# Four small gaps between the activation tiles of a two-block transformer kernel: what the on-chip addresses of matmul operands do to its time

## The chip, the cores and the metric

The kernel runs on one core of one Trainium2 chip, as one launch. The metric is the device time of that launch in microseconds (us), the median of the runs shown. Beside it stands one execution recorded by the hardware profiler, from which all rows below are read.

## What is computed

The reference runs two small transformer stacks, one behind the other, on 256 tokens of width 1024, all in float32. The first has two layers, each with two gated feed-forward layers (FFN) around a mixer (a short convolution in layer 0, a three-branch sparse attention in layer 1). The second has two layers with a mixer each.

```python
def swiglu_ffn(x, w_in, w_out):
    gate, up = jnp.split(x @ w_in, 2, axis=-1)
    return (jax.nn.silu(gate) * up) @ w_out
...
    for i in range(DEPTH):
        if i == N_A_LAYERS:
            kv = shared_kv(h, kv_norm, w_kv, k_norm, ...)
        h = h + 0.5 * swiglu_ffn(rmsnorm(h, ffn1_norm[i]), ffn1_w_in[i], ffn1_w_out[i])
        hn = rmsnorm(h, mix_norm[i])
        if i < N_A_LAYERS:
            h = h + short_conv_mixer(hn, conv_w_in[i], conv_w[i], conv_w_out[i])
        else:
            h = h + nsa_mixer(hn, attn_w_q[j], attn_q_norm[j], attn_w_o[j], rel_bias, kv)
        h = h + 0.5 * swiglu_ffn(rmsnorm(h, ffn2_norm[i]), ffn2_w_in[i], ffn2_w_out[i])
...
    for layer in range(DEPTH):
        h = rms_norm(x, pre_norm[layer])
        m = even_mixer(...) if layer % 2 == 0 else odd_mixer(...)
        x = x + rms_norm(m, post_norm[layer])
```

The feed-forward width is 2816, so each of the four FFNs multiplies 256 x 1024 by 1024 x 5632 and 256 x 2816 by 2816 x 1024. Every other large product (`conv_w_in`, `w_kv`, `attn_w_q`, `w_in_even`, `w_in_odd` and the matching output matrices) has 1024 rows too.

## The kernel before

The activations stay on the chip for the whole program, features on the partitions and tokens along the free axis: `hres` holds the residual as 8 tiles of 128 x 256. The weights are streamed from device memory, each once, through two rings of two slots: `raw_a` for the input matrices (a chunk is 1024 x 256), `raw_b` for the rows of the output matrices (a chunk is 128 x 1024).

**Three products for one.** TensorE takes its operands as fp32r, which keeps fewer bits than float32. To keep the precision, each operand is split into a high part (a rounded copy) and a low part (the rest). The weights are split on the chip: ScalarE writes `wah` (line 1098) and `wbh` (1105), VectorE writes `wal` (1494, 1665), and GpSimd writes `wbl` (2046; VectorE at 1749 in the mixers). The activations are split as well: ScalarE writes `hnh` (1166), VectorE `hnl` (1512, 1548), `hidh` (1547) and `hidl` (1548). One product is then three matmuls, which the helper `mm3` issues on lines 644 to 646:

```python
mm(dst, wh, xh, start=start, stop=False)   # L644: high weights, high activations
mm(dst, wh, xl, start=False, stop=False)   # L645: high weights, low activations
return mm(dst, wl, xh, start=False, stop=stop)  # L646: low weights, high activations
```

Here the weights are the stationary operand, 128 x 128 each, loaded afresh for each matmul by a LDWEIGHTS; the activations are the moving operand, 128 x 256. So in each triple TensorE reads a 512-byte stretch of each partition of a weight tile, and streams a 1024-byte stretch of an activation tile. In the jobs of kind "N" of the projections the roles are exchanged: `hnh`/`hnl` are stationary and `wah`/`wal` are moving.

**An FFN** has 22 chunks. For each, `up` makes gate and up parts (2 groups x 8 row tiles, 16 triples) from `hnh`, `hnl`, `wah`, `wal` into PSUM bank 4 or 5, and `down` adds one chunk of hidden features to the residual's 8 accumulators (8 triples) from `hidh`, `hidl`, `wbh`, `wbl`. `up` of a chunk goes ahead of `down` of the chunk before. That is 24 triples, or 72 matmuls, a chunk. Between them VectorE scales the sums (1600), ScalarE applies silu (1204), and VectorE multiplies (1604) and splits (1547, 1548). The convolution has the same form with 8 chunks. The projections (`project`) run `mm3` over 5 to 16 chunks; attention (`attend`) works with plain float32 matmuls (832, 833, 850 to 852, 868, 869), with two more bf16 matmuls on a tile of zeros (874) at each step of the first attention. All waits are semaphores between hand-written engine programs; there is no scheduler.

**Where the tiles stand.** On-chip tensors are declared with the helper `sb(...)` at the top of `build`. They are placed in that order from byte 16,512 of each partition on, and each start is rounded up to a multiple of 32 bytes. The weight tiles come early, the split activations late: `wah`, `wal`, `wbh`, `wbl`, `hres`, `sqs`, `cst`, `arena`, `t384`, ..., `tmp`, `gate_hid`, then `hidh`, `hidl`, `hnh`, `hnl`, and behind them `zero`, `rms`, `pbuf`, `ptb` and the small tiles of the softmax.

Of the kernel before, what the change touches and what calls it, by code (L numbers as in the profile page):

```python
# [18 lines left out]
F32R = mybir.dt.float32r  # L19
# [6 lines left out]
P = 128  # L26
T = 256
D = 1024
KT = D // P
# [72 lines left out]
def build(nc, a, out):  # L102
    ctx = ExitStack()
    with ctx:
        def sb(name, shape, dt=F32):
            return ctx.enter_context(nc.sbuf_tensor(name, shape, dt))
# [38 lines left out]
        tmp = sb("tmp", [P, 2, 512])  # L145
        gate_hid = sb("gate_hid", [P, 4, T])
        silu, hf = gate_hid[:, 0:2], gate_hid[:, 2:4]
        hidh, hidl = sb("hidh", [P, 2, T], F32R), sb("hidl", [P, 2, T], F32R)
        hnh, hnl = sb("hnh", [P, KT, T], F32R), sb("hnl", [P, KT, T], F32R)
        zero = sb("zero", [P, 512], BF16)  # L150
        rms = sb("rms", [P, T + 2])
        rtok, rln = rms[:, 0:2], rms[:, 2:T + 2]
# [2006 lines left out]
```

## Time and profile before

| | us |
|---|---|
| runs of the kernel before | 1530.22, 1530.47, 1540.99 |
| their median | 1530.47 |
| the profiled execution's own time | 1530.22 |
| its span, from the first to the last instruction | 1528.1 |
| TensorE busy with matmuls in the span | 1428.9 |
| VectorE, ScalarE, GpSimd busy | 900.4, 631.7, 435.2 |

The profiled execution is one of the three runs. Its time is its span and 2.1 us around it. Engines run at the same time, so their busy times don't add up. PE is TensorE's matmul row, PEld its weight loads, DVE is VectorE, ACT is ScalarE, POOL is GpSimd. Matmuls are pipelined, so that one of some 280 ns starts every 113 to 118 ns; what a matmul costs in a dense stretch is the distance between two starts, not its own duration.

### The profile page before, as it was taken

What the parts mean: (1) busy time and instruction counts of PE and PEld (TensorE: products, weight loads), DVE (VectorE), ACT (ScalarE), POOL (GpSimd) and SP (SyncE); (2) the same over time, 40 slices, a digit from 0 to 9 for tenths busy, and PEclk for the clock granted to TensorE, in tenths of its full rate; (3) what the DMA queues carried; (4) which work ended last, traced back from release to release, by engine and by line L of the source; (5) the groups of instructions that cost most, each with busy time, mean ns of one, the idle gap of its engine ahead of it and who ended that gap; (6) DMA issues with size and microseconds to landing.
All of it is one profiled execution on the core that took longest, in us unless ns stands there. A gap on an engine that the chain in (4) does not pass through costs nothing.

```text
span 1528.1 us, 28008 instructions
## 1 busy us (share of the span) xinstructions
PE 1428.9 (94%) x10980; PEld 1319.2 (86%) x11011; DVE 900.4 (59%) x1406; ACT 631.7 (41%) x954; POOL 435.2 (28%) x226
## 2 busy tenths in 40 slices
PE   4999999999999999999979999999999998799767
PEld 4999999989999989999965557999999986698646
DVE  3784568775455554545665663745455696573764
ACT  3443353354334353434434553534342434434442
POOL 1354431124443414444213440344430003000310
PEclk8999999999999899999976999999999997999788
DMA  7778646657765456666330102666643541353002
GB/s 205 209 211 236 191 140 191 178 181 233 218 184 174 125 159 188 183 188 183 124 104 23 32 22 70 196 186 196 200 143 99 164 145 34 123 166 111 28 1 83
DMA packets 271773, 222.55 MB, mean 146 GB/s; under 512 B 8082, under 2 KB 252326, under 8 KB 271580
## 3 DMA queue, kind: packets, MB, share of 16 engines
q1 hardware_dynamic: 268176, 212.44, 45.9%
q0 software_dynamic: 2368, 7.60, 2.2%
q10 hardware_dynamic: 1164, 1.62, 0.3%
q8 instruction: 43, 0.70, 0.2%
q14 instruction: 22, 0.18, 0.0%
HBM read 216.40 MB, written 4.19 MB: 144 GB/s over the span
## 4 chain that ended last, share of the span: by engine, by line
PE 77%; DVE 13%; ACT 5%; DMA 2%; issue 2%; ACTq 0%; another core or an unknown queue 0%; DVEq 0%; SPq 0%
PE bank L644 21%; PE bank L645 20%; PE bank L646 20%; PE bank L832 2%; DVE wal L1494 2%; PE bank L874 2%; PE bank L868 2%; DVE rstd L1476 2%; ACT wah L1098 1%; DVE wal L1665 1%; PE bank L833 1%; PE bank L850 1%; ACT hnh L1166 1%; DMA raw_a<-in_ffn_w_in 1%; PE bank L911 1%
## 5 line engine op out<-in xcount | busy, mean ns | idle before, releaser
L644 PE MATMUL bank<-hnh,wah 128*128 128x256 f32 (+1 forms) x2080 | 589.1, 283 | 8.5 <-DVE wal L1494 6.4
L2046 POOL TENSOR_TENSOR wbl<-raw_b,wbh 128x1024 fp32r<-128x1024 f32 x102 | 337.7, 3312 | 883.4 <-ACT wbh L1105 787.5
L645 PE MATMUL bank<-hnl,wah 128*128 128x256 f32 (+1 forms) x2080 | 581.0, 279 | 0.0
L646 PE MATMUL bank<-hnh,wal 128*128 128x256 f32 (+1 forms) x2080 | 580.8, 279 | 0.0
L644 PEld LDWEIGHTS bank<-hnh,wah 128*128 128x128 f32 (+1 forms) x2080 | 395.6, 190 | 10.3 <-issue 4.0
L645 PEld LDWEIGHTS bank<-hnl,wah 128*128 128x128 f32 (+1 forms) x2080 | 393.3, 189 | 2.1 <-issue 1.4
L646 PEld LDWEIGHTS bank<-hnh,wal 128*128 128x128 f32 (+1 forms) x2080 | 393.6, 189 | 0.0
L1494 DVE TENSOR_TENSOR wal<-raw_a,wah 128x2048 fp32r<-128x2048 f32 (+1 forms) x129 | 297.8, 2308 | 121.8 <-ACT wah L1098 120.9
L1098 ACT ACTIVATE wah<-raw_a 128x2048 fp32r<-128x2048 f32 (+3 forms) x127 | 239.0, 1885 | 85.5 <-PE bank L646 63.8
L644 PE MATMUL bank<-hidh,wbh 128*128 128x256 f32 x768 | 216.4, 282 | 2.0 <-DVE hidl L1548 2.0
L1204 ACT ACTIVATE gate_hid<-tmp 128x256 f32<-128x256 f32 x88 | 36.9, 419 | 426.8 <-DVE tmp L1600 426.8
L645 PE MATMUL bank<-hidl,wbh 128*128 128x256 f32 x768 | 213.3, 278 | 0.0
L646 PE MATMUL bank<-hidh,wbl 128*128 128x256 f32 x768 | 213.2, 278 | 0.0
L1600 DVE TENSOR_TENSOR tmp<-bank,rms 128x512 f32<-128x512 f32 x88 | 60.9, 692 | 220.1 <-PE bank L646 210.8
L1105 ACT ACTIVATE wbh<-raw_b 128x1024 fp32r<-128x1024 f32 x120 | 125.6, 1049 | 62.5 <-PE bank L646 37.6
L644 PEld LDWEIGHTS bank<-hidh,wbh 128*128 128x128 f32 x768 | 145.3, 189 | 2.4 <-DVE hidl L1548 2.4
L645 PEld LDWEIGHTS bank<-hidl,wbh 128*128 128x128 f32 x768 | 144.2, 188 | 0.4
L646 PEld LDWEIGHTS bank<-hidh,wbl 128*128 128x128 f32 x768 | 144.3, 188 | 0.0
L2118 POOL TENSOR_SCALAR pbuf<-pbuf,rs 128x256 f32<-128x256 f32 (+1 forms) x72 | 64.0, 889 | 88.0 <-DVE rs L1722 63.8
L1315 ACT ACTIVATE pbuf<-pbuf,nmx 128x128 f32<-128x128 f32 (+2 forms) x144 | 59.5, 415 | 41.3 <-DVE nmx L1707 35.3
L1604 DVE TENSOR_TENSOR gate_hid<-gate_hid,tmp 128x256 f32<-128x256 f32 x88 | 39.9, 453 | 42.9 <-ACT gate_hid L1204 42.9
L832 PE MATMUL bank<-arena 64*128 64x256 f32 (+1 forms) x112 | 47.1, 533 | 18.8 <-DVEq L1947 8.8
(237 smaller groups left out, 1827.5 us busy)
## 6 DMA issues: line engine op xcount, KB each, us to landing
raw_a<-in_ffn_w_in SPq DMA_DIRECT2D x176, 512.0 KB, 5.1
raw_b<-in_ffn_w_out SPq DMA_DIRECT2D x88, 512.0 KB, 4.8
raw_a<-in_w_in_even SPq DMA_DIRECT2D x15, 1024.0 KB, 5.3
raw_a<-in_conv_w_in SPq DMA_DIRECT2D x24, 512.0 KB, 4.3
raw_a<-in_w_in_odd SPq DMA_DIRECT2D x11, 1024.0 KB, 5.3
raw_a<-in_w_kv SPq DMA_DIRECT2D x6, 1024.0 KB, 5.0
raw_b<-in_conv_w_out SPq DMA_DIRECT2D x8, 512.0 KB, 5.7
raw_a<-in_attn_w_q SPq DMA_DIRECT2D x4, 1024.0 KB, 5.9
```

What stands on the lines that cost most here:

```text
L644: mm(dst, wh, xh, start=start, stop=False)
L645: mm(dst, wh, xl, start=False, stop=False)
L646: return mm(dst, wl, xh, start=False, stop=stop)
L832: mm(b[:, 0:T], m["q"][:, P:T], m["k"], start=True, stop=True)
L1098: act.activation(wah[:, s, :, 0:w], raw_a[:, wa.slot(u), :, 0:w], ACT.Copy).then_inc(S("a_hi"), 1)
L1105: act.activation(wbh[:, s], raw_b[:, s], ACT.Copy).then_inc(S("b_hi"), 1)
L1315: x = act.activation(pbuf[:, r, lo:hi], pbuf[:, r, lo:hi], ACT.Exp, bias=nmx[:, r, i:i + 1], accum_out=sm[:, r, i:i + 1])
L1494: v.tensor_tensor(wal[:, s, :, 0:w], raw_a[:, (n["ra"] + u) % 2, :, 0:w], wah[:, s, :, 0:w].bitcast(F32), ALU.subtract).then_inc(S("a_lo"), 1)
L1600: v.tensor_tensor(tmp[:, gs, :].rearrange("p (g c) -> p g c", g=2), bank[4 + gs][:, :].rearrange("p (g c) -> p g c", g=2), rln[:, None, :] ...
L1604: link(v.tensor_tensor(hf[:, hs, :], silu[:, gs, :], tmp[:, gs, T:2 * T], ALU.mult))
L2046: g.tensor_tensor(wbl[:, s], raw_b[:, s], wbh[:, s].bitcast(F32), ALU.subtract).then_inc(S("b_lo"), 1)
L2118: g.tensor_scalar(pbuf[:, r, lo:hi], pbuf[:, r, lo:hi], rs[:, r, 1:2], None, ALU.mult).then_inc(S("p1_scaled"), 1)
```

## The change

Four tensors that nothing reads or writes are declared between the split activations. They take 64, 96, 32 and 384 bytes of each partition.

```diff
-        hidh, hidl = sb("hidh", [P, 2, T], F32R), sb("hidl", [P, 2, T], F32R)
-        hnh, hnl = sb("hnh", [P, KT, T], F32R), sb("hnl", [P, KT, T], F32R)
+        sb("gap0", [P, 16])
+        hidh = sb("hidh", [P, 2, T], F32R)
+        sb("gap1", [P, 24])
+        hidl = sb("hidl", [P, 2, T], F32R)
+        sb("gap2", [P, 8])
+        hnh = sb("hnh", [P, KT, T], F32R)
+        sb("gap3", [P, 96])
+        hnl = sb("hnl", [P, KT, T], F32R)
```

No instruction is added, removed or moved on any engine; only start addresses differ. These are the starts in bytes of each partition in the two built programs, and their distances to the weight tiles. The four weight tiles all start at 128 bytes past a multiple of 2048, so one distance serves for all four.

```
tile            before    after     distance to the weight tiles, modulo 2048
wah              41088    41088
wal              57472    57472
wbh              73856    73856
wbl              82048    82048
hidh            187200   187264     704 before,  768 after
hidl            189248   189408     704 before,  864 after
hnh             191296   191488     704 before,  896 after
hnl             199488   200064     704 before, 1280 after
zero            207680   208256
rms             208704   209280
pbuf            209760   210336
ptb             220512   221088
```

Within these tiles the reads step by 512 bytes (stationary blocks) and 1024 bytes (moving tiles), so what stays fixed is the distance modulo 512: 192 bytes for all four before, and 256, 352, 384 and 256 bytes after. Every tensor behind `hnl` stands 576 bytes (9 x 64) later. These tiles do not move and come up in the prediction: `hres` at 90240, `cst` at 100480, `arena` at 110752, `t384` at 155808, `tmp` at 179008, `gate_hid` at 183104.

## Rows read from the trace of the kernel before

**Rows 1.** The page's head: busy time of each engine, its share and instructions

```profile
span 1528.1 us, 28008 instructions
PE 1428.9 (94%) x10980; PEld 1319.2 (86%) x11011; DVE 900.4 (59%) x1406; ACT 631.7 (41%) x954; POOL 435.2 (28%) x226
```

**Rows 2.** The chain of work that ended last, shares of the span

```profile
PE 77%; DVE 13%; ACT 5%; DMA 2%; issue 2%; ACTq 0%; another core or an unknown queue 0%; DVEq 0%; SPq 0%
```

**Rows 3.** Costliest groups of TensorE by form: shape, count | busy us, mean ns | idle before, releasers

```profile
L644 PE MATMUL bank<-hnh,wah 128*128 128x256 f32 x2064 | 584.6, 283 | 7.5 <-DVE wal L1494 6.4 <-DVE wal L1665 1.0
L645 PE MATMUL bank<-hnl,wah 128*128 128x256 f32 x2064 | 576.5, 279 | 0.0
...
L644 PE MATMUL bank<-hidh,wbh 128*128 128x256 f32 x768 | 216.4, 282 | 2.0 <-DVE hidl L1548 2.0
L645 PE MATMUL bank<-hidl,wbh 128*128 128x256 f32 x768 | 213.3, 278 | 0.0
...
L645 PE MATMUL bank<-hnl,wbh 128*128 128x256 f32 x192 | 53.9, 280 | 0.0
```

**Rows 4.** Busy time by stretch: steady parts of the four FFNs, then the attention stages

```profile
60.00:200.00 140.00, 140.00 (x1238) 140.00 (x1237) 86.55 (x106) 55.29 (x55) 66.01 (x25) 1.00 0.73 212
340.00:480.00 140.00, 140.00 (x1237) 140.00 (x1237) 71.97 (x87) 55.31 (x53) 61.08 (x18) 1.00 0.71 212
580.00:740.00 160.00, 160.00 (x1361) 160.00 (x1360) 77.58 (x95) 59.23 (x57) 67.40 (x19) 1.00 0.62 187
980.00:1120.00 140.00, 140.00 (x1238) 140.00 (x1237) 72.79 (x86) 54.82 (x52) 63.42 (x18) 1.00 0.66 199
782.00:930.00 148.00, 136.41 (x616) 77.25 (x626) 89.57 (x300) 71.23 (x252) 53.01 (x62) 0.86 0.09 28
```

**Rows 5.** TensorE's groups in the third FFN, 580 to 740 us

```profile
L646 PE MATMUL bank<-hnh,wal 128*128 128x256 f32 x302 | 84.9, 281 | 0.0
L645 PE MATMUL bank<-hidl,wbh 128*128 128x256 f32 x152 | 42.7, 281 | 0.0
```

**Rows 6.** TensorE's groups in the first FFN, 60 to 200 us

```profile
L646 PE MATMUL bank<-hnh,wal 128*128 128x256 f32 x276 | 76.2, 276 | 0.0
L645 PE MATMUL bank<-hidl,wbh 128*128 128x256 f32 x137 | 37.8, 276 | 0.0
```

**Rows 7.** The same in two neighbouring stretches of the convolution, 256:265 and 268:288 us

```profile
L645 PE MATMUL bank<-hnl,wah 128*128 128x256 f32 x19 | 5.2, 276 | 0.0
...
L645 PE MATMUL bank<-hnl,wah 128*128 128x256 f32 x41 | 11.5, 281 | 0.0
```

**Rows 8.** Timeline, float32 matmuls back to back: start, us to the last end, count

```profile
33.27 1.89 PE L628 MATMUL bank<-arena,cst 128*128 128x256 f32 x8
...
1372.05 2.32 PE L1038 MATMUL bank<-arena,t 128*96 128x256 f32 x10
```

**Rows 9.** Length of one such matmul at line 1038, from its line's view

```profile
L1038 PE MATMUL bank<-arena,t x32: 379/379/379, 1372.1 to 1378.7; 128*96 128x256 f32 x32
```

**Rows 10.** VectorE's groups by form: three of 512 columns on tiles of different starts, and the splits

```profile
L1600 DVE TENSOR_TENSOR tmp<-bank,rms 128x512 f32<-128x512 f32 x88 | 60.9, 692 | 220.1 <-PE bank L646 210.8 <-PE bank L652 6.0 <-DVE wal L1494 1.5
L1548 DVE TENSOR_TENSOR hidl<-gate_hid,hidh 128x256 fp32r<-128x256 f32 x96 | 40.9, 426 | 3.3
...
L1538 DVE TENSOR_TENSOR arena<-bank,rms 128x512 f32<-128x512 f32 x28 | 19.4, 691 | 20.4 <-PE bank L646 18.9 <-DVE rms L1484 0.7
...
L1585 DVE TENSOR_TENSOR hres<-hres,tmp 128x512 f32<-128x512 f32 x8 | 5.5, 692 | 0.3
```

## The prediction

> **What bounds the kernel now.** I read the page's head first: TensorE has a matmul under way in 1428.9 of 1528.1 us, the next engine, VectorE, in 900.4 [rows 1]. The chain of work that ended last says the same from the other end: 77% of the span stands on TensorE, 13% on VectorE [rows 2]. The groups of TensorE show on what: the triples of lines 644 to 646, with `hnh`/`hnl` against `wah`/`wal` (2064 triples), with `hid` against `wb` (768) and with `hn` against `wb` (192), and almost no idle time ahead of them, 7.5 and 2.0 us in the two largest groups [rows 3]. With the 128 triples of the projections that have the roles exchanged and 16 narrow ones, that is about 3 x 3,150 = 9,450 matmuls. Whatever changes the distance between two of their starts by 1 ns changes the time by 9.5 us. The change can act there, because every one of these matmuls reads an activation tile whose distance to the weight tiles is new.
>
> **The pace of these matmuls.** The view by stretch gives it. In the steady parts of three FFNs 1,238, 1,237 and 1,238 matmuls stand in 140 us; the count takes in some two that began before the stretch, so a start comes every 140 / 1,235.5 = 113.3 ns. In the third FFN 1,361 stand in 160 us: 160 / 1,358.5 = 117.8 ns [rows 4]. The clock was granted in full in all four. So there are two paces, 4.5 ns apart. They also show in the duration of one: 281 ns in the third FFN [rows 5], 276 ns in the first [rows 6]. That makes a mean a ruler: over the whole program the low-part matmuls of `down` average 278 ns [rows 3], so (278 - 276) / (281 - 276) = 40% of them ran at the slow pace.
>
> **What the trace says of addresses.** Three readings bear on it.
>
> First, the four FFNs use the same tiles at the same addresses, and three have the fast pace and one the slow [rows 4]. In the convolution one stretch has 276 ns and the next 281 ns, again with the same tiles [rows 7]. So the pace is a state that a stretch falls into when it starts, and the distance between tiles does not decide it, at least not alone.
>
> Second, within a stretch the pace does not depend on which tiles are read. `up` and `down` read different tiles, and the stationary block steps by 512 bytes against a moving tile that stays. Both have 281 ns in the slow stretch [rows 5] and both have 276 ns in the fast one [rows 6]. This covers steps of 512 bytes and more. It does not cover finer ones: all four activation tiles now stand at 192 bytes modulo 512 from the weights, and the change moves them to 256, 352, 384 and 256.
>
> Third, for fine distances the nearest rows are float32 matmuls. Line 628 streams `sqm` (in `arena`, tile 36, byte 147,616) against the ones in `cst` (byte 100,992): 46,624 bytes, 32 modulo 128. Eight take 1.89 us from the first start to the last end. Line 1038 streams `dq` (in `arena`, tile 16, byte 127,136) against blocks of `uq` (`t384`, from byte 155,808 in steps of 384): 28,672 bytes and more, in steps of 384, always 0 modulo 128, as `hidh`, `hnh` and `hnl` will have it. Ten take 2.32 us [rows 8]. With 379 ns for the last one [rows 9], the starts lie (1.89 - 0.38) / 7 = 216 ns and (2.32 - 0.38) / 9 = 216 ns apart. A moving stream with weight loads beside it goes at one speed at both distances. The weight load has more time to hide there than in a triple (216 ns against 113), so this is evidence and no proof.
>
> **The change part by part.** The two programs have the same instructions in the same order, so there is no count of added work.
> - *The triples.* Value taken: 0 ns each, from the three readings. Bounds: if all of them took the slow pace, the 60% that are now fast would pay 4.5 ns: 0.6 x 9,450 x 4.5 = +25.5 us. If all took the fast pace: 0.4 x 9,450 x 4.5 = -17.0 us. Still lower lies the float32 pass: 216 ns for a float32 matmul of 256 columns that streams them twice is 108 ns a pass, and against the mean of 0.6 x 113.3 + 0.4 x 117.8 = 115.1 that would be 9,450 x 7.1 = -67 us. Nothing shows a triple at that pace, so I keep it as the far end only.
> - *VectorE and ScalarE on the moved tiles.* Value taken: 0. A tensor_tensor of 512 columns takes 692 ns into `tmp` (byte 179,008, 64 modulo 128), 691 ns into `arena` (32 modulo 128) and 692 ns into `hres` (0 modulo 128) [rows 10], so the start's place modulo 128 does not matter to 1 ns. `hidl` at 32 modulo 64 is new, and `arena` has it already. Bounds: 1 ns either way over 300 instructions of the attention window on VectorE [rows 4], or 0.3 us. In the FFNs the split of 426 ns [rows 10] lies beside TensorE, which has no pause there in 140 us [rows 4].
> - *Tiles behind the gaps.* `pbuf`, `ptb`, `zero` and the small ones move by 576 bytes, a multiple of 64. TensorE reads `pbuf`, `ptb` and `zero` in attention; by rows 8 again 0.
>
> Sum: 1528.1 + 2.1 around the span + 0 = 1530.2 us, against a median of 1530.47 of the three runs.
>
> **What a run does by itself.** The sum would hold if the stages drew the same paces again. An FFN has 22 x 72 = 1,584 matmuls, so one that changes pace moves the time by 1,584 x 4.5 ns = 7.1 us. The profiled execution has one slow FFN of four. The run of 1540.99 us is 10.8 us longer than the profiled one, as much as one and a half FFNs. If the pace is drawn anew by each stretch, at 40% slow, the expected count is 1.6 of four, 0.6 more than profiled, or +4 us; two of three runs drew the better one. I take half of that: 1532 us.
>
> **Two places of the Trainium skill.** Its page "TensorE: Matmul & The Clock Gate", section "Back-to-back issue gap", puts the warm distance of two matmuls at N / 2.4 + 2.5 ns, an estimate of 109.2 ns for 256 columns. By that rule 4.1 ns a matmul is lost to something even at the fast pace, and a layout that gave it back would be worth some 39 us more than the fast rival below: 1474 us. The trace has no triple that fast, the loads being afresh each time. Against it speaks "SBUF — State Buffer", section "Who interferes with whom": TensorE has one read port for the moving operand and an independent one for LDWEIGHTS. By this rule no distance can matter, and the sum stays at 1530 us. The equal 216 ns of rows 8 agree with it; that the two paces exist at all is not explained by it.
>
> **The rivals.**
> 1. *Slower: the two read streams meet.* The mechanism is in the triples: the slow pace is the load of one block and the stream of another held up at the same part of the memory, and a distance of 0 modulo 128 makes it permanent. It decides where `hidh`, `hnh` and `hnl` come to stand at such a distance (768, 896, 1280), which is all of them but `hidl`. All triples at 117.8 ns: 1530.2 + 25.5 = 1556 us. For it: a slow pace exists, and 0 modulo 128 is untested in triples. Against it: rows 8 at the same distance, and the slow pace's presence at 192 modulo 512, where it comes and goes.
> 2. *Faster: the common distance was the bad one.* With four different distances the streams no longer fall into step and each stretch takes the fast pace: 1530.2 - 17.0 = 1513 us. For it: all four tiles share one distance now, so a stretch that falls into step stays so for 1,440 matmuls. Against it: three of four FFNs have the fast pace at that distance.
> 3. *No lasting effect, but a worse draw.* Three or four slow FFNs in the middle run: 1530.2 + 3 x 7.1 = 1552 us. It needs two of three runs to be so.
>
> **How the numbers follow.** No effect of the layout, with the draw near that of before: 0.74, at 1532 us, its own range 1522 to 1546. Rival 1: 0.11. Rival 2, with its far end by the float32 pass: 0.10. Rival 3: 0.05. The range of 1517 to 1549 holds nearly all of the first case and the near edges of the rivals, and leaves out the 1556 and the 1513. A measurement of this kernel can tell about 1% from no change, which is 15 us: 1515 to 1546. Slower by more than that is most of rivals 1 and 3 (0.14); faster is rival 2 at full size (0.09); within 1% the rest (0.77).
>
> **What would show it right or wrong.** Right: the four FFN stretches show 1,237 or 1,238 matmuls in 140 us, or about 1,189 (140 / 117.8), and nothing else; some have the one and some the other; L1600 and the splits keep 692 and 426 ns; idle time ahead of L644 stays under 10 us. Wrong, rival 1: all four FFNs at 281 ns, and in a repeat as well. Wrong, rival 2: no stretch at 281 ns, the projections included. Wrong in kind: a third pace, say 109 or 122 ns, or a pace that differs between `up` and `down` within one stretch, since that could only come from the distances.

## The result, and the profile after

The changed kernel takes 1562.48 us (median of 4 runs, 1562.28 to 1564.36). The kernel before, run again beside it, has 1535.73 us (4 runs, 1530.22 to 1543.82). The ratio is 1.0165, with a 95% interval of 1.0124 to 1.0206: slower, by 1.65%, and outside the range of the forecast (1517 to 1549). Medians here and below are of all runs, while ratios and their intervals leave out slow runs, those over 1.5% above the fastest of the same kernel. The profiled execution took 1562.44 us, with a span of 1560.3, which is 32.2 us more than before.

The page's head, the chain's shares and the costliest groups of TensorE by form, of the changed kernel (its lines stand 6 later: L650 to L652 are the triple of L644 to L646):

```profile
span 1560.3 us, 28039 instructions
PE 1466.3 (94%) x11011; PEld 1351.9 (87%) x11011; DVE 899.3 (58%) x1406; ACT 631.1 (40%) x954; POOL 435.4 (28%) x226
...
PE 81%; DVE 11%; ACT 4%; DMA 2%; issue 2%; ACTq 0%; DVEq 0%; SPq 0%
```

```profile
L650 PE MATMUL bank<-hnh,wah 128*128 128x256 f32 x2064 | 593.8, 288 | 2.5 <-DVE wal L1500 2.1 <-DVE wal L1671 0.4
L652 PE MATMUL bank<-hnh,wal 128*128 128x256 f32 x2064 | 586.6, 284 | 0.0
L651 PE MATMUL bank<-hnl,wah 128*128 128x256 f32 x2064 | 581.9, 282 | 0.0
L650 PE MATMUL bank<-hidh,wbh 128*128 128x256 f32 x768 | 218.6, 285 | 2.7 <-DVE hidl L1554 2.7
```

TensorE alone has grown: VectorE, ScalarE and GpSimd are busy as long as before to 1.1 us [rows 1], and TensorE's share of the chain went from 77 to 81% [rows 2]. The `hnh,wah` group averages 288 ns for 283 [rows 3], and the idle time ahead of it fell from 7.5 to 2.5 us, since a slower TensorE is waited for more and waits less. The 31 matmuls more in the count are records that the trace of before lacks.

The stretches of the four FFNs (columns: stretch, its length, PE, PEld, DVE, ACT and POOL busy with counts, granted clock, DMA share, GB/s):

```profile
60.00:200.00 140.00, 140.00 (x1182) 140.00 (x1181) 82.61 (x102) 52.93 (x54) 62.37 (x24) 1.00 0.69 203
340.00:480.00 140.00, 140.00 (x1181) 140.00 (x1181) 70.35 (x85) 53.91 (x51) 59.22 (x17) 1.00 0.69 206
600.00:760.00 160.00, 160.00 (x1351) 160.00 (x1350) 78.38 (x95) 60.31 (x57) 66.09 (x19) 1.00 0.60 180
1010.00:1150.00 140.00, 140.00 (x1182) 140.00 (x1181) 67.86 (x84) 52.44 (x50) 56.79 (x16) 1.00 0.61 184
```

Against 1,238 in 140 us before [rows 4] there are 1,182: 140 / 1,179.5 = 118.7 ns from start to start, and the same in all four. No stretch has 113.3 ns. Within a stretch, `up` and `down` now differ, which they did not before [rows 5, 6]. The groups of the first FFN, 60 to 200 us:

```profile
L652 PE MATMUL bank<-hnh,wal 128*128 128x256 f32 x262 | 74.2, 283 | 0.0
L651 PE MATMUL bank<-hnl,wah 128*128 128x256 f32 x261 | 73.3, 281 | 0.0
L651 PE MATMUL bank<-hidl,wbh 128*128 128x256 f32 x133 | 37.3, 280 | 0.0
```

The starts in the trace give `up` 119.1 ns and `down` 118.0 ns. Summed over all starts of triples that lie 100 to 150 ns apart, they are 15.6 us over an even 113.33 ns a matmul before, and 51.6 us after. That is +36.0 us in the triples; the pauses between them shrink by 4.7 us, and what remains (+0.9 us) lies outside. So the 32.2 us are found, and the added time lies in the matmuls whose operands the gaps moved.

VectorE paid nothing as a whole. Its rows of 512 columns and the split on the moved tile (512 columns at L1606 and L1544, the split at L1554):

```profile
L1606 DVE TENSOR_TENSOR tmp<-bank,rms 128x512 f32<-128x512 f32 x88 | 60.9, 692 | 244.1 <-PE bank L652 236.2 <-PE bank L658 5.5 <-DVE wal L1500 0.8
L1554 DVE TENSOR_TENSOR hidl<-gate_hid,hidh 128x256 fp32r<-128x256 f32 x96 | 40.9, 426 | 3.3
L1544 DVE TENSOR_TENSOR arena<-bank,rms 128x512 f32<-128x512 f32 x28 | 19.3, 691 | 22.1 <-PE bank L652 20.6 <-DVE rms L1490 0.7
```

All three are as in [rows 10], to the nanosecond. One row on a moved tile does differ, the rounded copy into `hidh`, before and after:

```profile
L1547 DVE CAST hidh<-gate_hid 128x256 fp32r<-128x256 f32 x96 | 34.5, 359 | 8.9
...
L1553 DVE CAST hidh<-gate_hid 128x256 fp32r<-128x256 f32 x96 | 36.4, 379 | 8.9
```

The 20 ns do not go with the address: in the kernels further down the same row has 380 ns with `hidh` at its old byte (hid_undone) and 336 ns with it at the changed kernel's byte (hn_undone). TensorE has no pause there.

### The profile page after: what moved, and what is told of

It reads as the page before. It is cut to its first block, busy times and chain, and to the rows that moved or that the text cites. A ratio compares the mean times of both kernels' runs of the same rounds, so it can differ in the third digit from the quotient of the medians.

```text
span 1560.3 us, 28039 instructions
## 1 busy us (share of the span) xinstructions
PE 1466.3 (94%) x11011; PEld 1351.9 (87%) x11011; DVE 899.3 (58%) x1406; ACT 631.1 (40%) x954; POOL 435.4 (28%) x226
## 4 chain that ended last, share of the span: by engine, by line
PE 81%; DVE 11%; ACT 4%; DMA 2%; issue 2%; ACTq 0%; DVEq 0%; SPq 0%
PE bank L650 22%; PE bank L652 22%; PE bank L651 21%; PE bank L838 2%; DVE wal L1500 2%; PE bank L880 2%; PE bank L874 2%; DVE rstd L1482 2%; ACT wah L1104 1%; PE bank L839 1%; PE bank L856 1%; PE bank L875 1%; DMA raw_a<-in_ffn_w_in 1%; PE bank L877 1%; PE bank L917 1%
## 5 line engine op out<-in xcount | busy, mean ns | idle before, releaser
L650 PE MATMUL bank<-hnh,wah 128*128 128x256 f32 (+1 forms) x2080 | 598.3, 288 | 3.4 <-DVE wal L1500 2.1
L652 PE MATMUL bank<-hnh,wal 128*128 128x256 f32 (+1 forms) x2080 | 591.1, 284 | 0.0
L650 PEld LDWEIGHTS bank<-hnh,wah 128*128 128x128 f32 (+1 forms) x2080 | 395.8, 190 | 8.5 <-issue 3.7
L652 PEld LDWEIGHTS bank<-hnh,wal 128*128 128x128 f32 (+1 forms) x2080 | 393.6, 189 | 0.0
L650 PE MATMUL bank<-hidh,wbh 128*128 128x256 f32 x768 | 218.6, 285 | 2.7 <-DVE hidl L1554 2.7
L652 PE MATMUL bank<-hidh,wbl 128*128 128x256 f32 x768 | 215.2, 280 | 0.0
L1606 DVE TENSOR_TENSOR tmp<-bank,rms 128x512 f32<-128x512 f32 x88 | 60.9, 692 | 244.1 <-PE bank L652 236.2
L650 PEld LDWEIGHTS bank<-hidh,wbh 128*128 128x128 f32 x768 | 144.8, 189 | 3.1 <-DVE hidl L1554 3.1
L652 PEld LDWEIGHTS bank<-hidh,wbl 128*128 128x128 f32 x768 | 145.0, 189 | 0.0
```

Source lines behind the costliest of these rows:

```text
L1606: v.tensor_tensor(tmp[:, gs, :].rearrange("p (g c) -> p g c", g=2), bank[4 + gs][:, :].rearrange("p (g c) -> p g c", g=2), rln[:, None, :] ...
```

## The experiments

Two kinds of kernel were run: the whole network with another layout, timed against the kernel before in the same session, and a measuring program that leaves the network out and runs only TensorE stretches at chosen distances (distance: start of the moving tile less start of the stationary block, in bytes). Each measuring program was executed once. The main loop of the first measuring program:

```python
for i, (wo, xo) in enumerate(SWEEP):        # element offsets; their difference is the distance
    if i:
        pe.wait_ge(given, i)                # one small ScalarE copy between two stretches
    for n in range(COUNT):
        m = mm(b, w[:, wo:wo + P], x[:, xo:xo + T], start=n == 0, stop=n == COUNT - 1)
    m.then_inc(asked, 1)
```

### Distance or start address: pace_curve, shift_all, weights_moved

> A measuring program: it leaves out the whole network. After a warm-up, TensorE runs 128 stretches of 48 fp32r matmuls (128x128 stationary, 128x256 moving), each stretch with one fixed byte distance between the stationary block and the moving tile: 0 to 2016 bytes in steps of 32, in a mixed order, first with the stationary block at byte 32,896, then 96 bytes later. Theory A (the distance between the two read streams sets the pace): the start-to-start time of a stretch is a function of the distance, some values at 113 ns and others at 118 to 123 ns, and the two halves give the same function; 704 is among the fast ones, 768, 864, 896 and 1280 among the slow ones. Theory B (the moving tile's own start address sets it): the second half's curve is that of the first moved by 96 bytes. Theory C (the draw at the start of a stretch alone, as forecast): 113.3 or 117.8 in no order, with no relation between the halves.

The timeline of five stretches, each cut off inside (start, us to the last end, count). In this order: distance 704, 896, 768, 864, and 1280, the last with the stationary block 96 bytes later:

```profile
219.57 3.93 PE L70 MATMUL bank<-x,w 128*128 128x256 f32 x32
307.17 3.96 PE L70 MATMUL bank<-x,w 128*128 128x256 f32 x32
382.27 4.00 PE L70 MATMUL bank<-x,w 128*128 128x256 f32 x32
425.99 3.88 PE L70 MATMUL bank<-x,w 128*128 128x256 f32 x31
482.28 3.88 PE L70 MATMUL bank<-x,w 128*128 128x256 f32 x31
```

With 0.28 us for the last matmul: 3.65 / 31 = 117.7 ns at 704, 3.68 / 31 = 118.7 at 896, 3.72 / 31 = 120.0 at 768, 3.60 / 30 = 120.0 at 864 and 1280. The whole curve, in ns from start to start, is the same eight numbers over and over from 0 to 2016 bytes:

```
distance modulo 256      0    32    64    96   128   160   192   224
block at byte 32,896   120.0 117.8 117.8 120.0 118.7 117.3 117.8 118.3
block at byte 32,992   120.0 116.7 117.8 120.0 118.7 117.3 117.8 118.3
```

(Mean of the last 40 starts of a stretch; each of the eight repeats in eight periods within 0.1 ns.) The distance sets the pace, and it counts modulo 256. The start address by itself does little: of the sixteen values only the one at 32 differs between the halves, by 1 ns. Of theory A one part failed: 704 showed 117.8 and not 113.3.

shift_all, against the kernel before:

```diff
+        sb("gap", [P, 48])
         raw_a = sb("raw_a", [P, 2, KT, T])
```

> One gap of 192 bytes ahead of the first tensor, the four gaps left out: all tiles stand 192 bytes later, all distances stay at 704 modulo 2048, and hnh starts at the very byte (191,488) where the changed kernel has it. Theory A (distance): as the kernel before, 1530 to 1544 us, FFN stretches at 113.3 or 117.8 ns. Theory B (own start address): the triples with hnh go to about 120 ns as in the changed kernel, 1550 to 1562 us.

Measured: 1533.40 us (10 runs, 1529.29 to 1548.15), ratio 0.9995 (0.9963 to 1.0026). Theory A holds: `hnh` at the very byte of the changed kernel costs nothing as long as the weights moved along. The FFN stretches show the two paces of before; the first and the third:

```profile
60.00:200.00 140.00, 140.00 (x1238) 140.00 (x1237) 87.00 (x106) 55.21 (x55) 66.72 (x25) 1.00 0.72 214
...
600.00:740.00 140.00, 140.00 (x1191) 140.00 (x1190) 67.53 (x84) 52.02 (x50) 58.20 (x17) 1.00 0.62 187
```

weights_moved, against the kernel before:

```diff
+        w2k = sb("w2k", [P, P])
+        w2v = sb("w2v", [P, 64])
+        rb = sb("rb", [33, 16])
         raw_a = sb("raw_a", [P, 2, KT, T])
...
-        rb = sb("rb", [33, 16])
...
-        w2k = sb("w2k", [P, P])
-        w2v = sb("w2v", [P, 64])
```

> w2k, w2v and rb (832 bytes) are declared ahead of the weight tiles and not behind them: the weights start 832 bytes later, the activations at the same bytes as in the kernel before; all four distances become 1920 modulo 2048, which is 896 modulo 1024, hnh's in the changed kernel. Theory A (distance): the pace of the triples rises to about 120 ns in up and down alike, 1570 to 1580 us (9,450 x 5 ns more than before). Theory B (own start address of the moving tile): as the kernel before, 1530 to 1544 us.

Measured: 1560.84 us (4 runs, 1559.91 to 1574.53), ratio 1.0196 (1.0126 to 1.0265). The split activations had not moved by a byte, and the triples slowed all the same. The pace was forecast a little too high (about 120 ns, and so 1570 us at least); the FFN stretch shows 118.7 ns, which is the curve's value at 128 modulo 256:

```profile
60.00:200.00 140.00, 140.00 (x1182) 140.00 (x1181) 82.43 (x102) 52.94 (x54) 61.99 (x24) 1.00 0.71 203
```

### Where the 113.3 ns come from: pace_phase

> The measuring program again, with the network left out: 192 stretches of 34 fp32r matmuls; distances 0 to 240 bytes in steps of 16, each tried behind 12 different leading float32 matmuls (none, or 2 to 512 columns), so that the stretch starts at another moment against the chip's clocks. The first curve has a period of 256 bytes and gave 117.8 ns at 192, where the kernel before has both 113.3 and 117.8. Theory A2 (distance and the start's moment together set the pace): 192 shows both 113.3 and 117.8 ns, depending on the leading matmul; 0, 96 and 128 never fall under 118 ns. Rival (the float of 113.3 comes from something else in the real kernel, such as the alternation of tiles): 192 stays at 117.8 behind every lead.

A lead is the float32 matmul that runs just ahead of a stretch. The timeline of three stretches, cut off inside: distance 192 with no lead, 192 behind a lead of 2 columns, 112 behind a lead of 190 columns:

```profile
51.82 2.88 PE L73 MATMUL bank<-x,w 128*128 128x256 f32 x24
...
126.41 2.75 PE L73 MATMUL bank<-x,w 128*128 128x256 f32 x22
...
650.82 2.66 PE L73 MATMUL bank<-x,w 128*128 128x256 f32 x22
```

That is 2.60 / 23 = 113.0, 2.47 / 21 = 117.6 and 2.38 / 21 = 113.3 ns. Over the 12 leads, distance 192 had the fast pace 6 times and the slow one 6 times, with nothing between: theory A2 holds in this, and the two paces are those that the kernel before has in its stretches. What picks one of the two is not known: with no lead, this program and pace_fine have 113.3 ns at 192, while pace_curve, with no lead either, has 117.8 ns in all its 16 stretches at 192 modulo 256. Distances 0, 96 and 128 never fell under 118.5. One distance had the fast pace behind all 12 leads: 112, which no 32-byte rounding of starts would hit. The others of the 16 lay between 116.6 and 120.2.

### Gaps that are multiples of the period: gaps_256

Against the changed kernel:

```diff
-        sb("gap0", [P, 16])
+        sb("gap0", [P, 64])
         hidh = sb("hidh", [P, 2, T], F32R)
-        sb("gap1", [P, 24])
+        sb("gap1", [P, 64])
         hidl = sb("hidl", [P, 2, T], F32R)
-        sb("gap2", [P, 8])
+        sb("gap2", [P, 64])
         hnh = sb("hnh", [P, KT, T], F32R)
-        sb("gap3", [P, 96])
+        sb("gap3", [P, 128])
         hnl = sb("hnl", [P, KT, T], F32R)
```

> Four gaps again, but of 256, 256, 256 and 512 bytes: larger in all than those of the change, and they leave each distance at 192 modulo 256. If the distance counts modulo 256 (the measured curve's period), nothing changes: 1530 to 1544 us, triples at 113.3 or 117.8 ns. If the cost of the change came from the tiles being apart at all, from four different distances, or from the tiles behind them standing later: 1550 us or more.

Measured: a median of 1547.14 us (10 runs, 1530.00 to 1560.05), ratio 1.0015 (0.9958 to 1.0072), while the kernel before had 1539.45 in that session, up to 1554.23. The median lies between the two ranges that were expected, 3 us over the first; by the ratio, gaps twice as large in all as those of the change make no difference that can be told. The run-to-run spread is that of before, and so are the paces: two FFNs fast (1,238 in 140 us, the first like the second) and two slow (1,360 in 160 us and 1,191 in 140 us). The second to the fourth:

```profile
340.00:480.00 140.00, 140.00 (x1238) 140.00 (x1237) 71.95 (x87) 55.28 (x53) 61.02 (x18) 1.00 0.70 213
580.00:740.00 160.00, 160.00 (x1360) 160.00 (x1360) 78.45 (x95) 60.30 (x57) 66.30 (x20) 1.00 0.60 183
990.00:1130.00 140.00, 140.00 (x1191) 140.00 (x1190) 67.44 (x81) 50.73 (x48) 60.52 (x17) 1.00 0.61 185
```

### Undoing one half: hid_undone and hn_undone

Both against the changed kernel. First hid_undone:

```diff
-        sb("gap0", [P, 16])
         hidh = sb("hidh", [P, 2, T], F32R)
-        sb("gap1", [P, 24])
         hidl = sb("hidl", [P, 2, T], F32R)
-        sb("gap2", [P, 8])
+        sb("gap2", [P, 48])
         hnh = sb("hnh", [P, KT, T], F32R)
         sb("gap3", [P, 96])
```

> The changed kernel with hidh and hidl back at their bytes of before (192 modulo 256 from the weights); hnh, hnl and all tiles behind them stay exactly where the change puts them. If each tile's own distance counts, the triples with hnh/hnl keep their 119 to 120 ns and only the down triples (2,304 matmuls at 118.0 ns in the changed kernel) can fall to 113 to 118 ns: 1551 to 1562 us. If the two gaps at hid carry the cost (hidl is the one tile that starts at an odd multiple of 32 bytes): 1530 to 1544 us.

Measured: 1565.01 us (4 runs, 1562.53 to 1579.86), ratio 1.0201 (1.0142 to 1.0260). Nothing came back, not even the 0 to 7 us allowed for. `down`, though its two tiles were at 192 again, ran at 118.0 ns in the first FFN, as in the changed kernel (118.0). It starts behind an `up` of 48 matmuls at bad distances; its first two starts lie 123 ns apart, and then it keeps the slow pace of 192 (117 to 119 ns from start to start). The group of its low-part matmuls in the first FFN, with the 281 ns of the slow pace:

```profile
L649 PE MATMUL bank<-hidl,wbh 128*128 128x256 f32 x131 | 36.8, 281 | 0.0
```

Then hn_undone:

```diff
         sb("gap0", [P, 16])
         hidh = sb("hidh", [P, 2, T], F32R)
         sb("gap1", [P, 24])
         hidl = sb("hidl", [P, 2, T], F32R)
-        sb("gap2", [P, 8])
+        sb("gap2", [P, 24])
         hnh = sb("hnh", [P, KT, T], F32R)
-        sb("gap3", [P, 96])
         hnl = sb("hnl", [P, KT, T], F32R)
```

> The other half: hidh and hidl stay where the change puts them (768 and 864), hnh and hnl return to 192 modulo 256. If the costs of the tiles add up, this kernel pays what the first half did not: at most 2,304 matmuls x 3 ns = 7 us over the kernel before, 1537 to 1546 us. If the fast pace needs every tile of the stream at a good distance (each down breaks it for the up behind it), the FFN stretches stand at 117.8 ns throughout and only the convolution's and projections' long up stretches draw 113.3: 6,336 FFN matmuls x 4.5 ns x the share that was fast before, 1550 to 1560 us.

Measured: 1540.73 us (10 runs, 1538.85 to 1545.07), ratio 1.0000 (0.9971 to 1.0028). The time agrees with the additive branch, the mechanism with neither. The stretches of the first and of the third FFN:

```profile
60.00:200.00 140.00, 140.00 (x1206) 140.00 (x1206) 84.75 (x105) 55.47 (x55) 62.36 (x25) 1.00 0.72 210
...
600.00:740.00 140.00, 140.00 (x1206) 140.00 (x1205) 69.56 (x85) 53.90 (x51) 58.04 (x18) 1.00 0.63 190
```

All four have 1,206: 140 / 1,203.5 = 116.3 ns, a pace that no FFN of the kernel before shows. The starts give `down` 117.8 and `up` 115.6 on the mean. But no single `up` has 115.6: whole `up`s of 48 matmuls alternate, 113.4 ns in one and 117.7 in the next, without an exception in the four stretches. Two neighbours in the first FFN, 98.2 to 103.2 us and 106.5 to 111.6 us:

```profile
L650 PE MATMUL bank<-hnl,wah 128*128 128x256 f32 x15 | 4.1, 276 | 0.0
...
L650 PE MATMUL bank<-hnl,wah 128*128 128x256 f32 x15 | 4.2, 281 | 0.0
```

These are the two paces of distance 192. So behind each `down` at bad distances the `up` takes one of them anew, here in strict turns, and keeps it to its end. An FFN no longer stays at one pace, and the spread is smaller: 1538.85 to 1545.07 us in 10 runs with a granted clock of 0.949 to 0.957. The kernel before, in its ten runs of the session with a clock of 0.948 or more, had 1532 to 1544 us in nine and 1558 in one. By the sums over 113.33 ns a matmul, one execution each: before 15.6 us, hid gaps alone 27.5, hn gaps alone 51.7, both 51.6. The parts don't add up (12 and 36 us, and 36 together); the `hn` gaps have the whole cost by themselves.

### Pairs of distances: pace_triples

> The measuring program with the network's own triples (high weights with high activations, high with low, low with high; the block steps by 512 bytes per triple): all 81 pairs of distances for the high and the low activation tile out of 0, 32, 64, 96, 112, 128, 160, 192, 224 bytes, each behind two leads. If a triple's pace is the sum of what the single distances gave (two for the high tile, one for the low): 113.4 at (112, 112), 113.4 or 117.8 at (192, 192), 120 at (0, 96), 118.6 to 120 at (128, 0). If what one matmul loses shifts the next one against its load, the mixed pairs depart from that: the network shows 118.0 at (0, 96) where the sum says 120, and 119.1 at (128, 0); the program should then show the network's numbers.

In ns from start to start, mean of the last 21 matmuls of a stretch, first lead and second lead:

```
high, low distance:  (192,192)      (112,112)      (0,96)         (128,0)        (0,0)          (112,192)
                     113.3, 113.3   113.3, 113.3   117.8, 117.8   120.0, 120.0   120.0, 120.0   115.6, 115.6
```

Of 81 pairs only two have 113.3 ns, those with both tiles at 192 and both at 112, and one more stays at 115.6 behind both leads. At (0, 96), the changed kernel's `hid` tiles, the mean of the single distances would be 120 and the program has 117.8, as the network's `down` (118.0). So the pace of a triple is not the mean of its single distances. At (128, 0), `hn`'s, it has 120.0 against the network's 119.1; that `down` breaks in there is a likely reason, not a tested one. Two matmuls that lie 21 starts apart, at (192, 192) and at (0, 96), both with the first lead:

```profile
144.92 0.28 PE L79 MATMUL bank<-x,w 128*128 128x256 f32 x1
147.30 0.28 PE L79 MATMUL bank<-x,w 128*128 128x256 f32 x1
...
164.10 0.28 PE L79 MATMUL bank<-x,w 128*128 128x256 f32 x1
166.57 0.28 PE L79 MATMUL bank<-x,w 128*128 128x256 f32 x1
```

That is 2.38 / 21 = 113.3 and 2.47 / 21 = 117.6 ns.

### What takes part: pace_fine

> The measuring program: distances 0 to 248 bytes in steps of 8 behind three leads; then a stationary block of 64 columns in place of 128 at steps of 16; then plain float32 matmuls. If two read streams hinder each other, the extra over the best pace (up to 6.7 ns at a distance of 0) shrinks to about half with half the block to read, and keeps its dependence on the distance; float32 matmuls, whose load has twice the time to hide in, stay at 216 ns at all distances. If the extra comes from the moving tile alone, it stays as large with 64 columns, and float32 shows it twice (about 229 ns at 0).

The timeline of three stretches, cut off inside: a block of 64 columns at distance 0, the same at 192, plain float32 at 0:

```profile
491.83 2.88 PE L78 MATMUL bank<-x,w 128*64 128x256 f32 x24
...
509.75 3.02 PE L78 MATMUL bank<-x,w 128*64 128x256 f32 x24
...
639.72 5.56 PE L80 MATMUL bank<-x,w 128*128 128x256 f32 x25
```

Three readings. With plain float32 matmuls the rows started 215.8 ns apart at all 16 distances ((5.56 - 0.38) / 24 here; each matmul has two rows). With a block of 64 columns the range stayed (113.3 to 120.0 ns), but the curve was another: 113.3 at 0, where 128 columns have 120.0, and 119.0 at 192, where they have 113.3 in this program. This fits neither branch: the extra did not halve, and it cannot come from the moving tile alone, since only the stationary block had changed. And the 16 distances that are odd multiples of 8 bytes had 120 ns or more in nearly all of their 48 stretches: one has 118.2, the others 119.8 to 130.3.

### A layout at the fast distance: at_112

```diff
-        hidh, hidl = sb("hidh", [P, 2, T], F32R), sb("hidl", [P, 2, T], F32R)
-        hnh, hnl = sb("hnh", [P, KT, T], F32R), sb("hnl", [P, KT, T], F32R)
+        split_x = sb("split_x", [P, 44 + 20 * T], F32R)[:, 44:44 + 20 * T].rearrange("p (a t) -> p a t", t=T)
+        hidh, hidl, hnh, hnl = split_x[:, 0:2], split_x[:, 2:4], split_x[:, 4:12], split_x[:, 12:20]
```

> All four activation tiles start 176 bytes later than before, 112 modulo 256 from the weights, the distance that gave 113.4 ns behind every lead. If the curve holds in the network, every stretch of triples runs at 113.3 ns: the 40% of slow ones before gain 17 us against the profiled 1530, so 1512 to 1516 us, with a spread under 3 us from run to run. If the curve is one of the measuring program alone (one block read again and again), it stays at 1530 to 1560 us.

Measured: 1525.27 us (10 runs, 1520.84 to 1536.19), ratio 0.9926 (0.9888 to 0.9964). It beats both kernels, the one before by 0.7%, and in the profiled execution every FFN has the fast pace; the first and the third:

```profile
60.00:200.00 140.00, 140.00 (x1237) 140.00 (x1237) 86.91 (x106) 55.24 (x55) 67.21 (x25) 1.00 0.73 213
...
580.00:740.00 160.00, 160.00 (x1414) 160.00 (x1414) 80.05 (x98) 60.81 (x59) 71.34 (x20) 1.00 0.63 191
```

It is some 10 us short of what I expected, and its spread is 15 us, not 3. Two parts are found. In the triples 5.2 us over the even 113.33 ns are left, so the profiled execution gained 10.4 us there and not 17. Some of that lies in the jobs of kind "N", where the roles are exchanged: they now have the weights 144 modulo 256 behind the blocks, and ran at up to 120.0 ns (in the kernel before, at 64, they ran at 117.8). Some lies behind each pause, where the first ten starts or so are 113 to 120 ns apart before the fast pace is found. And the runs differ in the granted clock: 0.949 to 0.954 in the seven under 1528 us, 0.941 to 0.946 in the three at 1535 to 1536 us. So a second source of spread goes with the clock; only one of the ten runs has a trace, so the paces of the others are not known.

## Why the prediction was wrong

**What bounds the kernel, and what 1 ns is worth: right.** TensorE's triples set the end before and after, and 3.9 ns more a matmul (115.0 to 118.9 on the mean) made +36 us, of which the pauses gave back 5.

**The step that failed: "The triples. Value taken: 0 ns each".** It measured +3.9 ns each. The three readings under it were true as rows and did not carry the conclusion.
- The first, that the pace is a state that a stretch falls into "and the distance between tiles does not decide it, at least not alone": pace_phase shows that the same tiles can have two paces at 192. But that is a property of this distance (others, such as 16 and 128, have two paces as well, but both slow). At 0, 96 or 128 no stretch with a 128-column block had the fast pace. Two outcomes at one distance said nothing of other distances.
- The second, no difference between `up` and `down` and between steps of 512 bytes: the period is 256, so each comparison made there was one of a distance with itself. I had written that it does not cover finer steps, and then counted it as one of three readings for zero all the same. The kernel before had one other distance to look at: in the jobs of kind "N" the exchanged roles put the moving weights at 64 modulo 256. The five stretches there of more than 30 matmuls, 256 columns and full clock all ran at 117.8 ns, never at 113.3.
- The third, float32 rows at 0 modulo 128: pace_fine confirms it at 16 distances, and it does not carry over to the triples. The likely reason is that the load there has 216 ns to hide in and here no time to spare, as the last rows of this section show; no run tests it. One row was also read as one matmul: line 1038 issues 16 matmuls and has 32 rows, so a float32 matmul takes two rows of 216 ns. No triple of 256 moving columns had a pace under 113.3 ns in any run, so nothing bears out the far end of 108 ns.

**The rival that came true: the first, in the main.** "All triples at the slow pace", +25.5 us and 1556 us, is 6 us short of the 1562.48. It had the right sign and the right place, and a chance of 0.11. Its condition was off: not a distance of 0 modulo 128, but nearly any modulo 256 (only 112 and 192 showed the fast pace with 128-column blocks). So was its price: 118.9 ns on the mean and not 117.8, since other distances have paces of their own. The sign announced in the text, "a third pace [...] or a pace that differs between `up` and `down` within one stretch", is what the profile shows.

**The second rival: wrong for this change, right as a possibility.** There is a layout with the fast pace in every FFN, at_112. The distances of the change are not it: of the pairs tried, only those with both tiles at 112 or both at 192 have the fast pace.

**The draw of each run: supported, and not the whole of the spread.** Layouts with all tiles at 192 modulo 256 were profiled three times, with one slow FFN at 1530.22 us, one at 1533.86 (shift_all) and two at 1540.40 (gaps_256). And runs of the kernel before at the same granted clock still differ: 1532.41 us at 0.954 and 1542.49 at 0.955 in the session of hn_undone. The run of 1540.99 us itself has no trace. The 1532 us was a guess at the middle; the medians of the later sessions were 1535 to 1542. In at_112 the times go with the granted clock over 15 us, so not all of the spread is the draw.

**VectorE and the tiles behind the gaps: right, 0.** Rows of 692, 691 and 426 ns stayed, and the one that did not, the copy into `hidh`, does not follow the address. All that lies outside the triples and their pauses is +0.9 us, and gaps_256, with the tiles behind moved by 1,280 bytes, is at 1.0015.

**On the two places of the Trainium skill.** The rule of "SBUF — State Buffer", section "Who interferes with whom", that the moving operand and LDWEIGHTS have independent read ports, would leave no room for a distance to matter, as the prediction read it. The measured curve differs (113.3 to 120.0 ns in pace_phase, in stretches in which no other engine has more than one small copy), and the measurement decides. Whether it is the reads that meet is open, as said below. The 109.2 ns that "TensorE: Matmul & The Clock Gate", section "Back-to-back issue gap", gives for 256 columns were not met at any of the distances tried; the best is 113.3. That section gives its formula for a single matmul apart and says that it does not hold for a stream with loads, so the prediction's 1474 us had little to stand on.

**What stays open.** That the distance between the stationary block and the moving tile, modulo 256 bytes, sets the pace is shown: by the curve, by weights_moved and by shift_all. Why is not, and neither is what picks one of the two paces at 192. A hindrance of the two read streams, which both draw from the same memory while one block is loaded and the other streamed, fits the facts that the start address by itself does next to nothing and that the plain float32 matmuls show no effect. But the half-wide block should then have lost less, and it lost elsewhere instead. An experiment with the weights left in place, and no load at all, was not tried.

What the rows do show is how little room there is. In the projections of the kernel before some triples stream 4 columns and not 256. Two of their matmuls that lie 42 starts apart, at full clock:

```profile
1172.24 0.25 PE L646 MATMUL bank<-wah,hnl 128*128 128x4 f32 x1
1176.93 0.25 PE L646 MATMUL bank<-wah,hnl 128*128 128x4 f32 x1
```

That is 4.69 / 42 = 111.7 ns from start to start, with next to nothing to stream: with a fresh load of 128 columns for each, matmuls of 4 columns go only 1.6 ns faster than the fast pace. And with half a block to load, 256 moving columns still take 113.3 ns at the least (pace_fine). So neither side by itself gets far under 113.3 ns, and a small hindrance of either can show; a float32 row, with 215.8 ns, leaves the same load some 104 ns to spare, by these numbers an estimate.

## What to carry to other kernels

Where TensorE runs matmuls of 256 fp32r columns with a fresh 128-column load each, the byte distance between the two operands modulo 256 is a parameter of the kernel, worth up to 6% of such a stretch (120.0 ns against 113.3), and a new tensor of 32 bytes anywhere between them can change it. Keep all operand pairs of one stretch at the same good distance (here 112; 192 had the fast pace behind 6 of 12 leads), and after any edit of the layout read the count of matmuls in a fixed window before anything else. A row of another kind of matmul, or a comparison that moves the operands only by multiples of the period, is no evidence on this.

## What the runs showed of the hardware that was not expected

- The pace of the stream against the distance has a period of 256 bytes and takes few values: 113.3, 116.7, 117.8, 118.7 and 120.0 ns make up most of the curve.
- At distances that are odd multiples of 8 bytes it is about 120 ns or more in all but one of 48 stretches; steps of 16 bytes show the structure.
- One distance (192) has two stable paces, 113.3 and 117.8 ns. Which one a stretch takes changes with what ran just before it, and it can hold for 1,500 matmuls (the third FFN of the kernel before, 570 to 749 us).
- In hn_undone, with one bad pair in a repeating pattern, whole groups of 48 matmuls take the two paces in turns, 113.4 and 117.7 ns, and the ten runs lie within 6 us of each other.
